# Hybrid attention layer on one core: a weight split, copies, zero fills and the change of branch moved; the last block's exponentials map by map

## The chip, the core and the metric

The kernel runs on one core of a Trainium2 chip. The metric is the device time of one execution in microseconds (us); less is better. The engines are called PE (TensorE), DVE (VectorE), ACT (ScalarE), POOL (GpSimd) and SP (SyncE, which issues most DMAs). Each engine has its own instruction stream, taken in the order written; they meet only at semaphores (`wait_ge`, `then_inc`).

## What is computed

One encoder layer over 1024 tokens of width 1024, in float32. The part that matters here is the input projection and the first of two attention branches (A); the second (B, windowed) follows it at once.

```
h    = layer_norm(x)
proj = h @ w_in                       # qa ka va | qb kb vb | ga gb
# branch A: 8 heads, 2 maps m per head, 8 blocks of 128 queries, chunk-causal
s[m] = q[m] @ k[m]^T * scale + bias ;  s = where(mask, s, -1e30)
p[m] = exp(s[m] - max s[m]) / sum     # one row max and one row sum per map
attn = p[0] - lam * p[1]
o    = attn @ v                       # then a norm per head
# branch B: 16 query heads, 2 kv heads, window of 2 chunks, with sinks
merged = sigmoid(ga)*(ya @ w_branch_a) + sigmoid(gb)*(yb @ w_branch_b)
h = layer_norm(alpha*h + merged @ w_out)
h = layer_norm(alpha*h + relu(h @ w_ff1)**2 @ w_ff2)
```

## The kernel before

Every float32 operand of a matrix product is kept as a high part (rounded copy, made by ACT) and a low part (value minus high part, made by DVE or POOL), and a product is three matmuls: high·high, low·high, high·low (`three`, L588 to L590). The order of each engine's instructions is written out by hand.

**Projection.** `w_in` is taken in tiles of 128 columns (`TILES`: qa, ka, va of head 0, of head 1, ...). A tile needs a split: SP loads `w_raw`, ACT makes the high part (`split_weights` in the scalar block, L892), POOL the low part in four pieces (L1239). A tile has two halves of 512 tokens; each is a `group` of 24 matmuls on PE, which can be issued in two pieces of 12 (`HALVES` says how many pieces lie in a block). ACT and DVE empty the group's PSUM bank (`group_hi`: L910 for q, L914 for k, L921 for v; `qk_lo`, L1409).

**Start.** Tokens are normalised, transposed on PE (`turn_tokens(n)`, L642, n = 0 to 15, two banks), scaled by DVE into `h_full` (`tokens_full`, L1435), and split by ACT (`tokens_hi`, L947) and POOL (L1262, semaphore `h_lo`). PE's first groups wait for `h_lo` piece by piece.

**Branch A.** For head h and block i (step = 8h + i), PE issues: `block_a(0)`, the scores against keys 0 to 511, two maps (L694); one piece of a group of the next head's projection; from i = 4 on `block_a(1)`, the scores against the other keys; the transposes of the probabilities of the step before (`transposes`, L614); the product with v of the step before that (`attend_a`, L677, L678); then perhaps a second piece. One unit of scores is one map and one range of keys; three PSUM banks (`SC`) take the units in turn.

DVE adds the bias and takes the row maxima (L1551, one for each unit), joins the two maxima of a map and negates them (L1561, L1562, semaphore `max_ready`), makes the low part of transposed probabilities (`batch_lo`, L1387), combines the two maps (`combine`, L1525, L1526, L1529, semaphore `probs_ready`, for which PE's transposes wait) and sums the halves of the output (`sum_halves`, L1516). For i > 4 `combine` of the step before stands between the maxima of the first and the second range of keys; the one of i = 7 stands in the next head's block 0, behind its maxima:

```python
                        if c == 0 and i > 4:
                            combine(step - 1)
```

ACT does, in step i, `exp_a(h, i)` (two exponentials with row sums, L1015, semaphore `exp_done`), `group_hi` of the group that ended, `batch_hi` (high part of the transposed probabilities of the step before, L898, semaphore `tr_hi`), and `out_rows` (L1004, L1007). For i < 4 the exponentials come first, for i >= 4 after `batch_hi`:

```python
                    if i < 4:
                        exp_a(h, i)
```

Before the first scores of a head the high part of its queries is copied to the other 64 rows (`double_queries`, L930, semaphore `q_doubled`).

**From A to B.** In the first steps of B the last blocks of A are finished between B's steps. B's values `v_main` and `v_side` need zeros in places, which POOL writes (L1283 and L1299, semaphore `v_zero`), and ACT copies the transposed values (`batch_hi(("vb", 0, b))`).

Of the kernel before, what the change touches and what calls it, by code (L numbers as in the profile page):

```python
# [12 lines left out]
P = 128  # L13
# [115 lines left out]
def program(nc, x, ln_in_g, ln_in_b, rel_bias, w_in, lambda_q1, lambda_k1, lambda_q2, lambda_k2, subln_g, sinks,  # L129
# [6 lines left out]
    with ExitStack() as ctx:  # L136
# [92 lines left out]
        GEMM, SC, TR, PV = banks[0:2], banks[2:5], banks[5:7], banks[7]  # L229
        RING = [banks[2], banks[3], banks[4], banks[7]]  # L230
# [59 lines left out]
        v_zero = sem("v_zero")  # L290
        sink_set = sem("sink_set")
# [293 lines left out]
        def _(pe):  # L585
# [48 lines left out]
            def turn_tokens(n):  # L634

                half, kt = n // KT, n % KT
                if n >= 2:
                    pe.wait_ge(h_full_done, n - 1)
                for t in range(4):
                    if kt == 0:  # L640
                        pe.wait_ge(ln_done, 4 * half + t + 1)
                    mm = pe.transpose(TR[n % 2][:, t * P:(t + 1) * P], res[:, 4 * half + t, kt * P:(kt + 1) * P], ident[:, :])  # L642
                mm.then_inc(h_turned, 1)
# [5 lines left out]
            for n in range(KT):  # L649
                pe.wait_ge(h_lo, n + 1)  # L650
                group(0, 0, [n])
                if n < 4:
                    turn_tokens(n + 4)
            group(1, 0)
            for n in (KT, KT + 1):
                turn_tokens(n)
            for kt in range(0, KT, 2):
                group(2, 0, range(kt, kt + 2))
                turn_tokens(KT + 2 + kt // 2)
            for kt in range(KT):  # L660
                pe.wait_ge(h_lo, KT + kt + 1)
                group(0, 1, [kt])
                if kt < 2:
                    turn_tokens(KT + 6 + kt)
# [16 lines left out]
            for h in range(A_HEADS):  # L681
                at = 0
                for i in range(NT):
# [3 lines left out]
                    def block_a(c):  # L687
                        keys = slice(c * HALF, min((c + 1) * HALF, (i + 1) * P))
                        for m in range(2):
# [43 lines left out]
            def attend_b(s):  # L733
                i = s % NT
                pe.wait_ge(tr_lo, BATCH[("pb", s, 1 if i else 0)] + 1)
                if s == 0:
                    pe.wait_ge(v_zero, 4)
# [144 lines left out]
        def _(act):  # L882
# [98 lines left out]
            for n in range(KT, 2 * KT):  # L981
                tokens_hi(n)
                if n in (KT + 1, KT + 6):
                    group_hi(1 + (n - KT) // 6, 0)
# [34 lines left out]
            double_queries(0)  # L1019
            act.wait_ge(spilled, 16 * NT)  # L1020
            for h in range(A_HEADS):
                at = 0
                for i in range(NT):
                    step = h * NT + i
                    if i < 4:
                        exp_a(h, i)
                    for piece in range(HALVES[i]):
# [4 lines left out]
                        if piece == 0:  # L1032
# [3 lines left out]
                            if i >= 4:  # L1036
# [9 lines left out]
                    splits_at = (1, 4, 5) if h == A_HEADS - 1 else (1, 4, 6)  # L1046
# [22 lines left out]
            for s in range(B_STEPS):  # L1069
                slot, first = s % 2, 0 if s % NT else CHUNK  # L1070
                act.wait_ge(max_ready, A_HEADS * NT + s + 1)
# [159 lines left out]
        def _(pool):  # L1231
# [36 lines left out]
            for n in range(FIRST, TILE[("qb", 1)] + 1):  # L1268
                split_weights(n)
# [105 lines left out]
        def _(dve):  # L1375
# [53 lines left out]
            def tokens_full(n):  # L1429
# [5 lines left out]
                dve.tensor_scalar(h_full[:, n % 4, :], TR[n % 2][:, :], gb_cols[:, kt:kt + 1], gb_cols[:, KT + kt:KT + kt + 1],  # L1435
# [97 lines left out]
            for h in range(A_HEADS):  # L1533
# [4 lines left out]
                for i in range(NT):  # L1538
# [6 lines left out]
                    for c in range(chunks):  # L1545
                        for m in range(2):
# [6 lines left out]
                                                     op0=ALU.add, op1=ALU.max, accum_out=mx[:, slot, m, c:c + 1]).then_inc(scores_read, 1)  # L1553
                        if c == 0 and i > 4:
# [4 lines left out]
                    dve.wait_ge(scores_read, SCORE[("a", h, i, 1, chunks - 1)] + 1)  # L1559
                    if chunks == 2:  # L1560
                        link(dve.tensor_tensor(mx[:, slot, :, 0], mx[:, slot, :, 0], mx[:, slot, :, 1], ALU.max))  # L1561
                    dve.tensor_scalar(neg_max[:, slot, :], mx[:, slot, :, 0], -1.0, None, ALU.mult).then_inc(max_ready, 1)  # L1562
# [31 lines left out]
            for s in range(B_STEPS):  # L1594
# [20 lines left out]
                if s == 0:  # L1615
                    combine(A_HEADS * NT - 1)
# [251 lines left out]
```

## Time and profile before

| | |
|---|---|
| median of 3 runs | 1809.54 us (1808.69 to 1810.73) |
| time of the profiled execution | 1807.46 us |
| its span, first to last instruction | 1805.7 us |
| busy: PE, DVE, ACT, POOL | 1766.9, 1085.4, 743.5, 661.9 us |
| mean granted TensorE clock | 0.997 |
| branch A with the next projections | about 66 to 517 us, 56 us for a head |
| branch B | about 517 to 700 us |

Times inside the execution are microseconds from the start of the span. Busy shares are averages over stages with different limits, so the argument is made from waits and from the order of instructions at one place. A matmul's end is modelled: consecutive matmuls of 512 columns start 0.23 us apart though each is recorded as 0.39 us.

### The profile page before, as it was taken

Reading aid. Unit: us, or ns where it says so; the run is one execution under the profiler, and the core shown is the slowest. Engines: PE = TensorE matmul, PEld = TensorE weight load, DVE = VectorE, ACT = ScalarE, POOL = GpSimd, SP = SyncE. Lnnn points to the kernel's source line nnn. Section 1 sums busy time; section 2 is a strip of 40 time slices with the busy share of each in tenths; the row PEclk is TensorE's granted clock in tenths of the full one; section 3 lists DMA queues with packets and bytes.
Section 4 is the critical chain, followed back from the end, with each engine's and each line's share of the span. In section 5 each row is a group of like instructions: output and inputs, shape, how many; then the busy total and the mean of one; then the engine's idle time right before and its main releaser. Section 6 shows DMA issues by size and latency. Waiting matters only on the chain.

```text
span 1805.7 us, 25434 instructions
## 1 busy us (share of the span) xinstructions
PE 1766.9 (98%) x8815; PEld 1476.3 (82%) x8815; DVE 1085.4 (60%) x2356; ACT 743.5 (41%) x1592; POOL 661.9 (37%) x662
## 2 busy tenths in 40 slices
PE   6999999999999999999999999999999999999998
PEld 4788888888878888888888888788888888888886
DVE  6477777777665553102423574777666667777667
ACT  5466666666556665210221132322233333222232
POOL 4311111121134443222222240555556656555570
PEclk9999999999999999999999999999999999999999
DMA  7311111111121101134232430211211111211212
GB/s 256 127 36 38 44 37 48 37 46 36 34 52 35 33 24 36 47 94 148 97 105 93 152 117 1 82 47 48 68 46 46 46 46 46 69 47 46 65 39 94
DMA packets 143399, 117.91 MB, mean 65 GB/s; under 512 B 23556, under 2 KB 130252, under 8 KB 143308
## 3 DMA queue, kind: packets, MB, share of 16 engines
q1 hardware_dynamic: 134092, 112.52, 20.3%
q10 hardware_dynamic: 9216, 4.20, 0.8%
q8 instruction: 54, 0.88, 0.2%
q14 instruction: 37, 0.30, 0.1%
HBM read 99.88 MB, written 21.53 MB: 67 GB/s over the span
## 4 chain that ended last, share of the span: by engine, by line
PE 88%; DVE 4%; ACT 3%; POOL 2%; issue 2%; DMA 0%; DVEq 0%; ACTq 0%; POOLq 0%
PE bank L588 26%; PE bank L590 26%; PE bank L589 26%; PE bank L614 4%; PE bank L694 3%; PE bank L677 2%; POOL w_lo L1239 1%; PE bank L625 1%; DVE mix L1551 1%; ACT mix L1015 1%; PE bank L678 1%; POOL hT_lo L1262 1%; ACT w_hi L892 1%; DVE mix L1529 0%; DVE small L1416 0%
## 5 line engine op out<-in xcount | busy, mean ns | idle before, releaser
L588 PE MATMUL bank<-hT_hi,w_hi 128*128 128x512 f32 x1296 | 515.1, 397 | 9.5 <-POOL w_lo L1239 4.9
L590 PE MATMUL bank<-hT_hi,w_lo 128*128 128x512 f32 x1296 | 506.8, 391 | 0.0
L589 PE MATMUL bank<-hT_lo,w_hi 128*128 128x512 f32 x1296 | 505.9, 390 | 0.0
L1239 POOL TENSOR_TENSOR w_lo<-w_raw,w_hi 128x256 fp32r<-128x256 f32 x260 | 185.5, 745 | 611.7 <-ACT w_hi L892 611.6
L588 PEld LDWEIGHTS bank<-hT_hi,w_hi 128*128 128x128 f32 x1296 | 244.1, 188 | 64.7 <-POOL hT_lo L1262 7.9
L590 PEld LDWEIGHTS bank<-hT_hi,w_lo 128*128 128x128 f32 x1296 | 243.9, 188 | 52.4
L589 PEld LDWEIGHTS bank<-hT_lo,w_hi 128*128 128x128 f32 x1296 | 244.3, 189 | 47.5
L588 PE MATMUL bank<-y_hi 128*128 128x512 f32 (+1 forms) x548 | 205.9, 376 | 0.8 <-issue 0.8
L589 PE MATMUL bank<-y_lo,y_hi 128*128 128x512 f32 (+1 forms) x548 | 203.2, 371 | 0.0
L590 PE MATMUL bank<-y_hi,y_lo 128*128 128x512 f32 (+1 forms) x548 | 203.2, 371 | 0.0
L1329 POOL TENSOR_TENSOR y_lo<-y_full,y_hi 128x512 fp32r<-128x512 f32 x98 | 131.8, 1373 | 165.9 <-ACT y_hi L1174 165.9
L1737 DVE SCALAR_TENSOR_TENSOR y_full<-bank,y_full 128x512 f32<-128x512 f32 x64 | 44.3, 692 | 187.0 <-ACT y_full L1171 187.0
L1772 DVE TENSOR_TENSOR res<-res,bank 128x512 f32<-128x512 f32 x208 | 132.5, 677 | 0.0
L1333 POOL TENSOR_TENSOR y_lo<-y_full,y_hi 128x512 fp32r<-128x512 f32 x98 | 125.5, 1306 | 16.7 <-DVE y_full L1740 16.7
L1551 DVE CUSTOM_DVE_ANT_0 mix<-bank,aux 128x512 f32<-128x512 f32 (+2 forms) x192 | 99.1, 552 | 48.6 <-PE bank L694 48.1
L1325 POOL TENSOR_TENSOR w_lo<-w_raw,w_hi 128x1024 fp32r<-128x1024 f32 x31 | 79.8, 2575 | 122.1 <-ACT w_hi L1166 122.1
L588 PEld LDWEIGHTS bank<-y_hi 128*128 128x128 f32 x548 | 103.0, 188 | 18.9 <-issue 1.2
L589 PEld LDWEIGHTS bank<-y_lo,y_hi 128*128 128x128 f32 x548 | 103.1, 188 | 17.8
L590 PEld LDWEIGHTS bank<-y_hi,y_lo 128*128 128x128 f32 x548 | 103.0, 188 | 17.8
L1174 ACT ACTIVATE y_hi<-y_full 128x512 fp32r<-128x512 f32 x98 | 54.2, 620 | 147.4 <-DVE y_full L1740 147.4
L1015 ACT ACTIVATE mix<-mix,small 128x256 f32<-128x256 f32 (+7 forms) x128 | 98.2, 769 | 37.7 <-DVE small L1562 36.9
L1740 DVE TENSOR_TENSOR y_full<-y_full 128x512 f32<-128x512 f32 x112 | 111.2, 1013 | 2.1
(202 smaller groups left out, 2992.3 us busy)
## 6 DMA issues: line engine op xcount, KB each, us to landing
w_raw<-in_w_in_dram SPq DMA_DIRECT2D x100, 256.0 KB, 3.3
w_raw<-in_w_ff_dram SPq DMA_DIRECT2D x64, 256.0 KB, 4.1
y_full<-in_w_ff_dram SPq DMA_DIRECT2D x32, 512.0 KB, 3.8
bias_rows<-bias_line SPq DMA_DIRECT2D x3, 1536.0 KB
res<-in_x_dram SPq DMA_DIRECT2D x8, 512.0 KB, 6.5
x_spill<-res SPq DMA_DIRECT2D x8, 512.0 KB, 6.0
o_spill<-o_buf ACTq DMA_DIRECT2D x64, 64.0 KB, 1.6
w_raw<-in_w_branch_b_dram SPq DMA_DIRECT2D x16, 256.0 KB, 3.9
```

Of the source, the lines that this page charges most:

```text
L588: pe.matmul(bank, lhs[0], rhs[0], start=start, stop=False)
L589: pe.matmul(bank, lhs[0], rhs[1], start=False, stop=False)
L590: return pe.matmul(bank, lhs[1], rhs[0], start=False, stop=stop)
L614: mm = pe.transpose(TR[n % 2][:, at * P:(at + 1) * P], src, ident[:, :])
L1015: e = act.activation(s_a[:, i % 2, m, 0:(i + 1) * P], s_a[:, i % 2, m, 0:(i + 1) * P], ACT.Exp, bias=neg_max[:, i % 2, m:m + 1], accum_out ...
L1239: ins = pool.tensor_tensor(w_tile(n, 1)[:, at:at + 2], w_raw[:, at:at + 2, :], w_tile(n, 0)[:, at:at + 2].bitcast(F32), ALU.subtract)
L1325: pool.tensor_tensor(w[1][:, n % 2], w_raw[:, :, :], w[0][:, n % 2].bitcast(F32), ALU.subtract).then_inc(w_lo_done, 1)
L1329: pool.tensor_tensor(w2[1][:, slot, :], w2_full[:, slot, :], w2[0][:, slot, :].bitcast(F32), ALU.subtract).then_inc(w2_lo, 1)
L1333: pool.tensor_tensor(u[1][:, slot, :], u_full[:, slot, :], u[0][:, slot, :].bitcast(F32), ALU.subtract).then_inc(u_lo, 1)
L1551: dve.tensor_tensor_reduce(out=s_a[:, slot, m, lo:hi], in0=SC[n % 3][:, 0:hi - lo], in1=bias_a[:, h % 2, off + lo:off + hi], scale=1.0, sc ...
L1740: dve.tensor_tensor(blocks[:, dst, :], blocks[:, a, :], blocks[:, b, :], op).then_inc(signal, 1)
L1772: ins = dve.tensor_tensor(total, total, bank, ALU.add)
```

## The change

1. **Start.** `turn_tokens` takes four PSUM banks in turn (`TURN = TR + SC[1:3]`) instead of two; in the first group's loop it stands ahead of the wait for `h_lo`, and four turns instead of two stand ahead of group 2. ACT empties group (2, 0) one token tile earlier.
2. **Copies.** `double_queries(0)` moves from behind `group_hi(2, 1)` to behind `group_hi(0, 1)`.
3. **Weight split.** Of the three splits in a head, ACT does the second at the end of block 3 instead of block 4.
4. **Last block of a head (i = 7).** PE issues the first map's second range of scores ahead of the group piece; DVE joins and negates the maxima of each map by itself; ACT's exponentials come at the head of the step, each waiting for its own map.
5. **Zeros.** `v_side[0]` is zeroed by POOL ahead of the split of tile vb, `v_side[1]` by DVE in step 0 of B (semaphore `side_zero`); the two POOL fills between A and B go.
6. **Branch change.** In B's step 1 ACT copies the transposed vb ahead of A's last `out_rows`.

```diff
+        TURN = TR + SC[1:3]
...
-                if n >= 2:
-                    pe.wait_ge(h_full_done, n - 1)
+                if n >= 4:
+                    pe.wait_ge(h_full_done, n - 3)
...
             for n in range(KT):
+                if n < 4:
+                    turn_tokens(n + 4)
                 pe.wait_ge(h_lo, n + 1)
                 group(0, 0, [n])
-                if n < 4:
-                    turn_tokens(n + 4)
...
                     block_a(0)
+                    if i == NT - 1:
+                        block_a(1, [0])
...
                             if i >= 4:
-                                block_a(1)
+                                block_a(1, range(i == NT - 1, 2))
...
             group_hi(0, 1)
+            double_queries(0)
             group_hi(1, 1)
...
             def exp_a(h, i):
-                act.wait_ge(max_ready, h * NT + i + 1)
                 for m in range(2):
+                    act.wait_ge(max_ready, 2 * (h * NT + i) + (m + 1 if i == NT - 1 else 2))
...
-                    if i < 4:
+                    if i < 4 or i == NT - 1:
                         exp_a(h, i)
...
-                            if i >= 4:
+                            if 4 <= i < NT - 1:
                                 exp_a(h, i)
...
-                    splits_at = (1, 4, 5) if h == A_HEADS - 1 else (1, 4, 6)
+                    splits_at = (1, 3, 5) if h == A_HEADS - 1 else (1, 3, 6)
...
                 if s == 1:
+                    act.wait_ge(side_zero, 2)
+                    for b in range(2):
+                        batch_hi(("vb", 0, b))
                     out_rows(A_HEADS * NT - 1, A_HEADS - 1, NT - 1)
                     store_rows(A_HEADS * NT - 1)
-                    act.wait_ge(v_zero, 2)
-                    for b in range(2):
-                        batch_hi(("vb", 0, b))
...
+                if n == TILE[("vb", 0)]:
+                    pool.memset(v_side[0].bitcast(F32), 0.0).then_inc(side_zero, 1)
                 split_weights(n)
...
-            pool.wait_ge(scores_read, SCORE[("b", 0, 0, 0, 0)])
-            for part in range(2):
-                pool.memset(v_side[part].bitcast(F32), 0.0).then_inc(v_zero, 1)
...
+                            if c and i == NT - 1:
+                                dve.wait_ge(scores_read, n + 1)
+                                link(dve.tensor_tensor(mx[:, slot, m, 0:1], mx[:, slot, m, 0:1], mx[:, slot, m, 1:2], ALU.max))
+                                dve.tensor_scalar(neg_max[:, slot, m:m + 1], mx[:, slot, m, 0:1], -1.0, None, ALU.mult).then_inc(max_ready, 1)
...
                 if s == 0:
+                    dve.memset(v_side[1].bitcast(F32), 0.0).then_inc(side_zero, 1)
                     combine(A_HEADS * NT - 1)
```

How the order of instructions moves, at two places. The first is ACT from the last block of head 0 to the first block of head 1 (`w_hi<-w_raw` is a split, `aux_49<-bank` the copy of va's second half, `y_lo<-bank` the two `batch_hi` of block 6, `mix,small<-mix,small` the exponentials, `o_buf` and `unused` `out_rows`). Before:

```order
L892 ACTIVATE w_hi<-w_raw 128x1024 [waits gemm_done,raw_loaded]
L921 ACTIVATE aux_49<-bank 128x512 [waits gemm_done]
L898 ACTIVATE y_lo<-bank 128x512 [waits tr_done]
L898 ACTIVATE y_lo<-bank 128x384 [waits tr_done]
L1015 ACTIVATE mix,small<-mix,small 128x1024 [waits max_ready]
L1015 ACTIVATE mix,small<-mix,small 128x1024
L1004 ACTIVATE o_buf<-o_buf,small 128x128 [waits o_stored1,inv_ready,pv_read]
```

Now:

```order
L894 ACTIVATE w_hi<-w_raw 128x1024 [waits gemm_done,raw_loaded]
L1018 ACTIVATE mix,small<-mix,small 128x1024 [waits max_ready] x2
L923 ACTIVATE aux_49<-bank 128x512 [waits gemm_done]
L900 ACTIVATE y_lo<-bank 128x512 [waits tr_done]
L900 ACTIVATE y_lo<-bank 128x384 [waits tr_done]
L1007 ACTIVATE o_buf<-o_buf,small 128x128 [waits o_stored1,inv_ready,pv_read]
```

The copy of va and both `batch_hi` stand behind the two exponentials, and each exponential has a wait of its own.

The second is DVE at the same place, from the maxima of the second range of keys to the combination of block 7 (`L1551` and `L1552` with `mix,small<-bank` are maxima, `y_lo<-bank,y_lo` the two `batch_lo` of block 6). Before:

```order
L1551 ISA mix,small<-bank,aux_50 128x512 [waits scores_done]
L1551 ISA small 128x1
L1561 TENSOR_TENSOR small<-small 128x2 [waits scores_read]
L1562 TENSOR_SCALAR small<-small 128x2 [waits dve_chain]
L1387 TENSOR_TENSOR y_lo<-bank,y_lo 128x512 [waits tr_hi]
L1387 TENSOR_TENSOR y_lo<-bank,y_lo 128x384 [waits tr_hi]
L1516 TENSOR_REDUCE o_buf<-bank 128x128 [waits sq_done,o_scaled,pv_done]
```

Now:

```order
L1557 TENSOR_TENSOR small<-small 128x1 [waits scores_read]
L1558 TENSOR_SCALAR small<-small 128x1 [waits dve_chain]
L1552 ISA mix,small<-bank,aux_50 128x512 [waits scores_done]
L1552 ISA small 128x1
L1557 TENSOR_TENSOR small<-small 128x1 [waits scores_read]
L1558 TENSOR_SCALAR small<-small 128x1 [waits dve_chain]
L1388 TENSOR_TENSOR y_lo<-bank,y_lo 128x512 [waits tr_hi]
L1388 TENSOR_TENSOR y_lo<-bank,y_lo 128x384 [waits tr_hi]
L1517 TENSOR_REDUCE o_buf<-bank 128x128 [waits sq_done,o_scaled,pv_done]
```

The pair that joins and negates maxima is there twice, one for each map; what follows it (`batch_lo` of block 6, the sum of halves, the next head's first maxima, then `combine` of block 7) keeps its order.

## Rows read from the trace of the kernel before

**Rows 1.** The page: busy time of the engines.
```profile
PE 1766.9 (98%) x8815; PEld 1476.3 (82%) x8815; DVE 1085.4 (60%) x2356; ACT 743.5 (41%) x1592; POOL 661.9 (37%) x662
```
**Rows 2.** PE's waits (line waited at, engine and line that released; total us, times, longest).
```profile
PE bank L588 <- POOL w_lo L1239: 4.9, 8, 0.6
PE bank L588 <- POOL hT_lo L1262: 4.4, 6, 1.4
PE bank L694 <- ACT y_hi L930: 2.9, 1, 2.9
PE bank L614 <- DVE y_lo L1387: 1.4, 2, 1.2
PE bank L614 <- DVE mix L1529: 0.8, 3, 0.3
```
**Rows 3.** PE's timeline, first scores of head 0 (start, length, idle before).
```profile
69.47 0.44 PE L694 MATMUL bank<-y_hi 128*128 128x128 f32 x1 [2.92 <-ACT y_hi L930]
...
74.28 0.28 PE L694 MATMUL bank<-y_hi 128*128 128x256 f32 x1
```
**Rows 4.** One stretch: length, busy (PE, PEld, DVE, ACT, POOL), PEclk, DMA share, GB/s.
```profile
69.40:72.80 3.40, 3.33 (x10) 2.87 (x11) 1.39 (x8) 0.88 (x4) 0.00 (x0) 0.50 0.55 204
```
**Rows 5.** ACT's timeline ahead of the first scores.
```profile
55.70 1.20 ACT L910 ACTIVATE y_hi<-bank 64x512 fp32r<-64x512 f32 x2 [2.37 <-PE bank L590]
61.15 0.59 ACT L914 ACTIVATE y_hi<-bank 64x512 fp32r<-64x512 f32 x1 [4.25 <-PE bank L590]
...
67.21 2.12 ACT L930 ACTIVATE y_hi<-y_hi 64x1024 fp32r<-64x1024 f32 x2
```
**Rows 6.** ACT's timeline, blocks 3 and 4 of head 1.
```profile
153.81 0.60 ACT L898 ACTIVATE p_more<-bank 128x512 fp32r<-128x512 f32 x1 [2.47 <-PE bank L614]
...
156.60 1.05 ACT L892 ACTIVATE w_hi<-w_raw 128x1024 fp32r<-128x1024 f32 x1
```
**Rows 7.** POOL's timeline in the start, second half of the tokens.
```profile
46.23 8.42 POOL L1262 TENSOR_TENSOR hT_lo<-mix,hT_hi 128x256 fp32r<-128x256 f32 x12 [2.04 <-ACT hT_hi L947]
```
**Rows 8.** The timeline, last block of head 1 into head 2.
```profile
177.03 0.68 DVE L1551 CUSTOM_DVE_ANT_0 mix<-bank,aux 128x512 f32<-128x512 f32 x1
177.54 0.98 ACT L898 ACTIVATE y_lo<-bank 128x512 fp32r<-128x512 f32 x2 [0.75 <-PE bank L614]
...
178.25 0.08 DVE L1551 DVE_READ_ACCUMULATOR2_ANT small<- 128x1 f32 x1
...
178.56 0.17 DVE L1562 TENSOR_SCALAR small<-small 128x2 f32<-128x2 f32 x1
178.63 1.15 DVE L1387 TENSOR_TENSOR y_lo<-bank,y_lo 128x512 fp32r<-128x512 f32 x2
...
178.76 1.15 ACT L1015 ACTIVATE mix<-mix,small 128x1024 f32<-128x1024 f32 x1 [0.24 <-DVE small L1562]
...
180.76 0.61 DVE L1562 TENSOR_SCALAR small<-small 128x2 f32<-128x2 f32 x1
...
181.04 0.39 ACT L1004 ACTIVATE o_buf<-o_buf,small 128x128 f32<-128x128 f32 x1
...
181.73 1.42 DVE L1529 SCALAR_TENSOR_TENSOR mix<-mix,small 128x512 f32<-128x512 f32 x2
...
182.53 1.32 PE L614 MATMUL bank<-ident,mix 128*128 128x128 f32 x8
183.22 1.26 ACT L898 ACTIVATE p_more<-bank 128x512 fp32r<-128x512 f32 x2 [0.64 <-PE bank L614]
...
183.86 1.35 DVE L1387 TENSOR_TENSOR p_more<-bank,p_more 128x512 fp32r<-128x512 f32 x2 [0.71 <-ACT p_more L898]
```
**Rows 9.** The timeline, from branch A to branch B.
```profile
514.92 0.95 POOL L1283 MEMSET y_hi<- 128x1024 f32 x1
...
515.04 1.75 DVE L1409 SCALAR_TENSOR_TENSOR y_lo<-bank,y_hi 128x512 fp32r<-128x512 f32 x1
...
516.87 0.33 PE L625 MATMUL bank<-y_hi 64*128 64x128 f32 x2 [0.93 <-DVE y_lo L1409]
```

More of the change, by code:

```diff
@@ L290, in program @@
         v_zero = sem("v_zero")
+        side_zero = sem("side_zero")
         sink_set = sem("sink_set")
@@ L641, in turn_tokens @@
                         pe.wait_ge(ln_done, 4 * half + t + 1)
-                    mm = pe.transpose(TR[n % 2][:, t * P:(t + 1) * P], res[:, 4 * half + t, kt * P:(kt + 1) * P], ident[:, :])
+                    mm = pe.transpose(TURN[n % 4][:, t * P:(t + 1) * P], res[:, 4 * half + t, kt * P:(kt + 1) * P], ident[:, :])
                 mm.then_inc(h_turned, 1)
@@ L649, in _ @@
             for n in range(KT):
+                if n < 4:
+                    turn_tokens(n + 4)
                 pe.wait_ge(h_lo, n + 1)
                 group(0, 0, [n])
-                if n < 4:
-                    turn_tokens(n + 4)
             group(1, 0)
-            for n in (KT, KT + 1):
+            for n in range(KT, KT + 4):
                 turn_tokens(n)
@@ L658, in _ @@
                 group(2, 0, range(kt, kt + 2))
-                turn_tokens(KT + 2 + kt // 2)
+                turn_tokens(KT + 4 + kt // 2)
             for kt in range(KT):
@@ L662, in _ @@
                 group(0, 1, [kt])
-                if kt < 2:
-                    turn_tokens(KT + 6 + kt)
             for n in (1, 2):
@@ L686, in _, with block_a @@
                         pe.wait_ge(q_doubled, h + 1)
-                    def block_a(c):
+                    def block_a(c, maps=range(2)):
                         keys = slice(c * HALF, min((c + 1) * HALF, (i + 1) * P))
-                        for m in range(2):
+                        for m in maps:
                             unit = SCORE[("a", h, i, m, c)]
@@ L736, in attend_b @@
                 if s == 0:
-                    pe.wait_ge(v_zero, 4)
+                    pe.wait_ge(v_zero, 2)
                     pe.wait_ge(pv_read, A_HEADS * NT)
@@ L982, in _ @@
                 tokens_hi(n)
-                if n in (KT + 1, KT + 6):
-                    group_hi(1 + (n - KT) // 6, 0)
+                if n in (KT + 1, KT + 5):
+                    group_hi(1 + (n - KT) // 5, 0)
             act.wait_ge(lam_dve, 1)
@@ L1017, in exp_a @@
                 e.then_inc(exp_done, 1)
-            double_queries(0)
             act.wait_ge(spilled, 16 * NT)
@@ L1070, in _ @@
                 slot, first = s % 2, 0 if s % NT else CHUNK
-                act.wait_ge(max_ready, A_HEADS * NT + s + 1)
+                act.wait_ge(max_ready, 2 * A_HEADS * NT + s + 1)
                 act.wait_ge(sink_set, s + 1)
@@ L1434, in tokens_full @@
                     dve.wait_ge(h_lo, n - 3)
-                dve.tensor_scalar(h_full[:, n % 4, :], TR[n % 2][:, :], gb_cols[:, kt:kt + 1], gb_cols[:, KT + kt:KT + kt + 1],
+                dve.tensor_scalar(h_full[:, n % 4, :], TURN[n % 4][:, :], gb_cols[:, kt:kt + 1], gb_cols[:, KT + kt:KT + kt + 1],
                                   ALU.mult, ALU.add).then_inc(h_full_done, 1)
@@ L1558, in _ @@
                             late = None
[L1559 to L1562, printed above, removed]
+                    if i < NT - 1:
+                        dve.wait_ge(scores_read, SCORE[("a", h, i, 1, chunks - 1)] + 1)
+                        if chunks == 2:
+                            link(dve.tensor_tensor(mx[:, slot, :, 0], mx[:, slot, :, 0], mx[:, slot, :, 1], ALU.max))
+                        dve.tensor_scalar(neg_max[:, slot, :], mx[:, slot, :, 0], -1.0, None, ALU.mult).then_inc(max_ready, 2)
                     if i == 0 and h:
```

## The prediction

> **What bounds the kernel now.** I read the page's busy times first: PE is busy in 1766.9 of 1805.7 us [rows 1], so only about 39 us of idle are there to win, and all the rest can only lose. Then PE's waits [rows 2]: they say which idle belongs to which of the six moves. 4.9 us in 8 waits are for the low part of a weight tile, 2.9 us in one wait for the copied queries, 4.4 us for `h_lo` in the start, 1.4 us for `batch_lo` near the change of branch (and 0.93 us more there [rows 9]), and 0.8 us in all are for `combine` at the ends of heads. Last the timelines at each place, for what stands ahead of and behind the moved instruction. The change aims at every one of these waits; the question is what it puts behind them.
>
> **Copies (part 2).** PE idles 2.92 us until 69.47 for the copies of L930, which ran from 67.21, behind the copy of va [rows 3, 5]. Their input is there after 56.9 us (55.70 + 1.20), and ACT then idles 4.25 us until 61.15 [rows 5]: the 2.12 us fit in whole, and nobody waits behind them. The weights' low part for the next group was ready at about the time PE stopped, so I leave 0.1 us of the wait: -2.8 us. After this gap the granted clock was 0.50 from 69.4 to 72.8 [rows 4], that is 1.2 instead of 2.4 GHz. From 69.47 to the next scores at 74.28 passed 4.81 us [rows 3]; the work between is 4 small and 12 large matmuls, at full clock about 4 x 0.11 + 12 x 0.23 = 3.2 us, so the low clock cost 1.6 us. Without the gap I expect no fall: -1.6. Together **-4.4 us** (bounds -2.8, if the fall comes anyway, and -4.5).
>
> **Weight split (part 3).** The 8 waits of 0.6 us [rows 2] are for a split that ACT begins at 156.60, at the end of block 4 [rows 6]. At the end of block 3 ACT idled 2.47 us until 153.81 [rows 6]; a split takes 1.05 us, so it fits, and POOL's 2.85 us behind it end some 5 us earlier. Its next load on SP's queue also moves earlier. **-4.9 us** (bounds 0, if another wait of PE takes its place, and -4.9).
>
> **Start (part 1).** PE's turns come earlier, but `h_lo` is what PE waits for [rows 2]. POOL makes the second half's low parts without a pause from 46.23 for 8.42 us, 1.4 us for each token tile, after a wait for ACT and not for PE [rows 7]; this run begins behind DVE's low part of group (1, 0), which keeps its place. The first half is held in the same way by DVE's statistics and a weight split. More banks for the turns don't shorten these chains: **0 us** (bounds -1, if DVE gets a turn earlier somewhere, and +1.6, one more fall of the clock, since PE's idle time is then gathered differently).
>
> **Last block (part 4), the term that decides.** The first map's maxima can't start earlier than now: on DVE they stand behind `combine` of block 6, which ends at 177.03 [rows 8], whatever PE does earlier. The pair of small instructions ends 0.40 us after the maxima (178.33 to 178.73) [rows 8]. So map 0 is ready at 177.71 + 0.40 = 178.11 and map 1 at 178.14 + 0.68 + 0.40 = 179.2. The two exponentials take 2.28 us (178.76 to 181.04) [rows 8]; they start at 178.14 and end at 180.42, 0.6 us earlier than now. That is the gain. The price: ACT's copy of va and both `batch_hi` of block 6 now stand behind them, and `batch_hi`, which started at 177.54 [rows 8], starts at 180.42 + 0.5 = 180.9. DVE is in order: its `batch_lo` of block 6, now at 178.63, begins 0.64 us after `batch_hi` (183.22 to 183.86) [rows 8], at 181.55, and the `combine` of block 7 stands behind it. From `batch_lo` to the combining instruction pass 3.10 us now (178.63 to 181.73), of which 0.4 us is one small instruction stretched from 0.17 to 0.61 us while POOL worked [rows 8]; I take 2.7, since POOL's work then lies elsewhere. So combining starts at 184.25 and PE's transposes, 0.80 us behind as now, at 185.05 instead of 182.53: **+2.5 us**. PE has nothing else to do in between: it arrives at these transposes at 182.2 to 182.5 in both programs, and its own stream is in order. The same end of a head comes 7 times: **+17.5 us** (bounds for one: 2.0, if `combine` catches up half a microsecond by not waiting for the exponentials, and 3.0, if the stretched instruction stays).
>
> **The clock behind these stalls.** A gap of 2.92 us was followed by 3.4 us at half clock, costing 1.6 us [rows 3, 4]; each head's end gets one of about 2.8 us. Gaps of up to 1.4 us [rows 2] were mostly not followed by one. I can't tell from one case how many of the seven will be; between none and all I take 3 (they come at changing times, and the one seen was slightly longer): 3 x 1.6 = **+4.8 us** (bounds 0 and 11.2).
>
> **Zeros and branch change (parts 5, 6).** At the end of head 7 DVE's low part of the qb group took 1.75 us beside POOL's zeros of 0.95 us each, and PE waited 0.93 us for it, until 516.87 [rows 9]; the zeros go. But ACT's copy of that same group also stands behind the exponentials now. Map 1 is ready about when L1409 starts now, at 515.04 [rows 9]; the exponentials end 1.2 us behind it (179.2 to 180.42 above), the copy and DVE's low part 1.3 us later (0.6 and 0.7), at 517.5: +0.7. DVE then does the 0.9 us fill of `v_side[1]` (I take POOL's 0.95 us) ahead of `combine` of block 63, for which PE had no wait before: +1.0. Copying vb ahead of `out_rows` saves ACT's 0.8 us of `out_rows` in the longest of the two L1387 waits (1.2 us) [rows 2]: -0.7. Together **+1.0 us** (bounds -1.8, if both old waits go, and +2.5). The fill of `v_side[0]` by POOL lies beside the last head, where DVE has idle time; I take 0 for it. The Trainium skill (SBUF — State Buffer, on the port pair that DVE and GpSimd share) says that the second of two such instructions is blocked for the whole of the first; by it the sum would be up to 0.9 us higher.
>
> **Sum.** -4.4 - 4.9 + 0 + 17.5 + 4.8 + 1.0 = +14.0 us on the profiled execution's 1807.46 us, 1821.5 us. The median of the runs shown is 2.1 us above that execution, so I forecast 1823.6 us.
>
> **Rivals.**
> 1. *Cover: the head ends cost nothing, and the kernel is faster.* Only the gains stay: -4.4 - 4.9, and about -1 at the branch change, 1799 us. For it speaks that exponentials end 0.6 us earlier and that PE's wait there is only 0.8 us in all now [rows 2]. It needs `batch_lo` of block 6 to be no later than about 179 us, that is, `batch_hi` not behind the exponentials. Against it: the listing of ACT's order shows it there, and the same rows show DVE in order. It decides as soon as the added wait of a head's end is under 1.3 us (9.3 / 7). Chance 0.10.
> 2. *Half price.* The wait grows by only 1 to 1.5 us, because DVE's steps between `batch_lo` and `combine` shrink when they no longer wait for anything: 7 x 1.3 = 9, no net change, 1807 to 1815 us. Against it: those steps are mostly work (1.15 us of `batch_lo`, the sum, two maxima, three small ones). Chance 0.10.
> 3. *The clock falls at every head end.* Forecast plus 4 x 1.6 = 1830 us, up to 1834 with 3.0 us a head. For it: the one long gap seen had a fall. Against it: shorter ones mostly had none. Chance 0.18.
> 4. *The split's wait doesn't go* (the raw tile comes too late for block 3): +4.9 on the forecast, 1828 us; the load is issued when POOL ends the split before, some 9 us earlier, and loads take 3.3 us. It lies inside the range; chance 0.05, counted with the forecast.
>
> **How the numbers follow.** The forecast, slower by the head ends, has 0.62; rival 3, 0.18; rival 2, 0.10; rival 1, 0.10. The range from 1813 (head ends at 2.0 us, no fall of the clock, and a little from the branch change) to 1835 (rival 3 with 3.0 us) leaves out rival 1 and most of rival 2. A measurement of this kernel can tell about 0.2%, 3.6 us, from no change. Faster by more: 0.11 (rival 1 and a little of rival 2). Within: 0.06, most of rival 2. Slower by more: 0.83.
>
> **What would show it.** Right: PE's waits list a new large entry, L616 (the transposes) for DVE's L1530, near 18 to 20 us in 7 or 8 waits of 2.5 to 3 us; the entries for POOL's L1239 and ACT's L930 are gone; ACT's `batch_hi` of block 6 starts after the second exponential; the mean clock is a little lower in branch A; head to head takes about 58 us instead of 56. Wrong: head to head takes 55.5 us and L616's wait stays under 1 us, or DVE's `batch_lo` of block 6 starts before 180.5 us on the scale of rows 8.

## The result, and the profile after

The changed kernel took **1820.5 us** (median of 4 runs, 1819.9 to 1824.8) against 1809.8 us for the kernel before on the same chip: ratio 1.0065, 95% interval [1.0047, 1.0082]. The forecast was 1823.6 us, with a range from 1813 to 1835. The profiled execution is the longest of the four: 1824.8 us, with a span of 1823.0 us and a mean granted clock of 0.989, where the others have 0.993 or 0.994. It is +17.3 us on the span of before; the medians differ by +10.7 us. That distance is a finding of its own (below).

The page's busy line, after:

```profile
PE 1775.7 (97%) x8815; PEld 1487.1 (82%) x8815; DVE 1080.4 (59%) x2373; ACT 742.7 (41%) x1592; POOL 660.4 (36%) x661
```

PE has as many matmuls as in [rows 1] and is busy 8.8 us longer. The granted clock, further down, shows where: this execution has 39 us at half clock, the one of before 9 us. PE's waits, after (total us, times, longest):

```profile
PE bank L616 <- DVE mix L1530: 18.6, 7, 2.7
PE bank L644 <- ACT res L944: 7.2, 4, 2.8
...
PE bank L590 <- POOL hT_lo L1264: 3.7, 7, 1.4
PE bank L627 <- DVE y_lo L1410: 1.6, 1, 1.6
```

Against [rows 2]: the 4.9 us for `w_lo` and the 2.9 us for the copies are gone, and 18.6 us for `combine` stand where 0.8 us stood. The timeline at the end of head 1, after (start, length, idle before; the place of [rows 8], where DVE's maxima of the first map began at 177.03):

```profile
174.80 0.68 DVE L1552 CUSTOM_DVE_ANT_0 mix<-bank,aux 128x512 f32<-128x512 f32 x1
...
175.90 1.15 ACT L1018 ACTIVATE mix<-mix,small 128x1024 f32<-128x1024 f32 x1 [5.01 <-DVE small L1558]
...
177.05 1.14 ACT L1018 ACTIVATE mix<-mix,small 128x1024 f32<-128x1024 f32 x1
...
178.18 0.57 ACT L923 ACTIVATE aux<-bank 128x512 f32<-128x512 f32 x1
...
178.66 0.96 ACT L900 ACTIVATE y_lo<-bank 128x512 fp32r<-128x512 f32 x2
...
179.27 1.16 DVE L1388 TENSOR_TENSOR y_lo<-bank,y_lo 128x512 fp32r<-128x512 f32 x2 [2.42 <-ACT y_lo L900]
...
182.03 1.42 DVE L1530 SCALAR_TENSOR_TENSOR mix<-mix,small 128x512 f32<-128x512 f32 x2
...
182.84 1.78 PE L616 MATMUL bank<-ident,mix 128*128 128x128 f32 x8 [2.66 <-DVE mix L1530]
```

Read from the maxima on, since the block as a whole lies at another time: ACT first idles 5.01 us for the first map, then does both exponentials, the copy of va and only then `batch_hi` (L900) (3.86 us behind the maxima; before, 177.54 - 177.03 = 0.51). DVE idles 2.42 us for it, does `batch_lo` (L1388), the sum, the next maxima and `combine` (L1530), and PE's transposes start 8.04 us behind the maxima instead of 5.50: +2.54 us, by the very chain of the prediction. All seven idle times at this place are 2.65 or 2.66 us.

The clock, seven windows of after, one at each head's end (length, busy of PE, PEld, DVE, ACT, POOL, then PEclk):

```profile
121.80:128.60 6.80, 6.19 (x28) 6.10 (x29) 4.33 (x11) 2.31 (x7) 0.00 (x0) 0.50 0.00 0
183.20:186.60 3.40, 3.40 (x18) 3.16 (x17) 2.19 (x6) 1.20 (x2) 0.00 (x0) 0.50 0.02 5
241.90:245.30 3.40, 3.24 (x26) 3.00 (x27) 2.61 (x7) 1.20 (x2) 0.00 (x0) 1.00 0.00 0
299.30:306.10 6.80, 6.28 (x28) 6.18 (x29) 4.33 (x12) 2.22 (x7) 0.00 (x0) 0.50 0.02 5
360.70:364.10 3.40, 3.40 (x18) 3.17 (x16) 2.18 (x6) 1.19 (x2) 0.00 (x0) 0.50 0.00 0
420.00:423.40 3.40, 3.39 (x27) 3.14 (x26) 2.61 (x8) 1.32 (x3) 0.00 (x0) 1.00 0.02 5
476.80:483.60 6.80, 6.30 (x28) 6.21 (x29) 4.33 (x12) 2.19 (x7) 0.00 (x0) 0.50 0.01 4
```

In this execution 5 of the 7 waits have half clock (1.2 GHz) behind them, three of them for 6.8 us. Outside these windows the clock was at half once near 30 us, once at the first scores of B (534.8) and at the very end. What that costs is read from PE's timeline, from the transposes of one head's last block to the next:

```profile
122.41 1.97 PE L616 MATMUL bank<-ident,mix 128*128 128x128 f32 x8 [2.65 <-DVE mix L1530]
...
242.05 1.32 PE L616 MATMUL bank<-ident,mix 128*128 128x128 f32 x8 [2.65 <-DVE mix L1530]
...
360.27 1.78 PE L616 MATMUL bank<-ident,mix 128*128 128x128 f32 x8 [2.66 <-DVE mix L1530]
419.52 1.32 PE L616 MATMUL bank<-ident,mix 128*128 128x128 f32 x8 [2.66 <-DVE mix L1530]
477.30 1.97 PE L616 MATMUL bank<-ident,mix 128*128 128x128 f32 x8 [2.66 <-DVE mix L1530]
```

From 360.27 to 419.52, with 3.4 us of half clock behind the first, pass 59.25 us; from 419.52 to 477.30, with none, 57.78. So a 3.4-us stretch costs 1.5 us. After a 6.8-us stretch (122.41 to the 182.84 above) it is 60.43: 2.7 us. The other heads repeat these three distances within 0.05 us.

### The profile page after: what moved, and what is told of

It is laid out like the page before. It is cut to its first block, busy times and chain, and to the rows that moved or that the text cites. A ratio compares the mean times of both kernels' runs of the same rounds, so it can differ in the third digit from the quotient of the medians.

```text
span 1823.0 us, 25506 instructions
## 1 busy us (share of the span) xinstructions
PE 1775.7 (97%) x8815; PEld 1487.1 (82%) x8815; DVE 1080.4 (59%) x2373; ACT 742.7 (41%) x1592; POOL 660.4 (36%) x661
## 4 chain that ended last, share of the span: by engine, by line
PE 89%; DVE 4%; ACT 3%; issue 2%; POOL 1%; DMA 0%; DVEq 0%; POOLq 0%; ACTq 0%
PE bank L590 26%; PE bank L592 26%; PE bank L591 26%; PE bank L616 4%; PE bank L694 3%; PE bank L677 2%; PE bank L627 1%; ACT mix L1018 1%; PE bank L678 1%; DVE mix L1552 1%; DVE mix L1530 1%; POOL hT_lo L1264 1%; DVE small L1527 0%; DVE y_lo L1388 0%; DVE small L1417 0%
## 5 line engine op out<-in xcount | busy, mean ns | idle before, releaser
L1552 DVE CUSTOM_DVE_ANT_0 mix<-bank,aux 128x512 f32<-128x512 f32 (+2 forms) x192 | 99.6, 552 | 43.8 <-PE bank L694 43.1
L1326 POOL TENSOR_TENSOR w_lo<-w_raw,w_hi 128x1024 fp32r<-128x1024 f32 x31 | 79.8, 2573 | 121.8 <-ACT w_hi L1168 121.8
L591 PEld LDWEIGHTS bank<-y_lo,y_hi 128*128 128x128 f32 x548 | 103.0, 188 | 17.8
L592 PEld LDWEIGHTS bank<-y_hi,y_lo 128*128 128x128 f32 x548 | 102.9, 188 | 17.8
```

The source lines that it names most:

```text
L591: pe.matmul(bank, lhs[0], rhs[1], start=False, stop=False)
L592: return pe.matmul(bank, lhs[1], rhs[0], start=False, stop=stop)
L1326: pool.tensor_tensor(w[1][:, n % 2], w_raw[:, :, :], w[0][:, n % 2].bitcast(F32), ALU.subtract).then_inc(w_lo_done, 1)
L1552: dve.tensor_tensor_reduce(out=s_a[:, slot, m, lo:hi], in0=SC[n % 3][:, 0:hi - lo], in1=bias_a[:, h % 2, off + lo:off + hi], scale=1.0, sc ...
```

## The experiments

Two theories stood against each other. **Theory 1**: the place of the exponentials in ACT's order sends `batch_hi`, then DVE's `batch_lo` and `combine`, then PE back. **Theory 2**: the work map by map does it (DVE's second pair of small instructions, PE's new order). What the other parts are worth was open beside that. Times are medians; ratios are to the kernel before on the same chip, whose median lay between 1809.0 and 1809.7 us.

### Undoing the suspected step, the whole part, and doing the part alone

`exp_behind`, the change with the exponentials of i = 7 behind `batch_hi` again and all else of part 4 kept:

```diff
-                    if i < 4 or i == NT - 1:
+                    if i < 4:
                         exp_a(h, i)
...
-                            if 4 <= i < NT - 1:
+                            if i >= 4:
                                 exp_a(h, i)
```

> The changed kernel with one thing undone: in a head's last block ACT does both exponentials behind the copies of the transposed probabilities again; the maxima are still joined map by map and PE still issues the first map's second scores early. Theory 1 (the price is the place of the copies behind the exponentials on ACT, and DVE's low parts behind them): PE's 7 waits of 2.7 us for the combined probabilities shrink to 0.4 us or less, the clock falls after them go, and the time is 1797 to 1801 us. Theory 2 (the price is DVE's added pair of small instructions, or PE's changed order, which let the maxima end later): the waits stay above 1.5 us and the time stays above 1812 us.

Measured: **1796.7 us**, ratio 0.9934 [0.9917, 0.9950], 24 us faster than the change and a little below the expected 1797. The waits at the heads' ends are 0.43 to 0.74 us, a little more than the 0.4 us expected; the one of 1.1 us in the row below lies at the change of branch, behind DVE's fill. `no_last`, the change without part 4 (those lines, PE's `block_a(1, [0])`, and DVE's pair for each map undone):

> The changed kernel without any of part 4 (last block as before: PE's order, joined maxima and exponentials), parts 1, 2, 3, 5 and 6 kept. Both theories: faster than before by the sum of the other parts. By the prediction's terms -4.4 (copies), -4.9 (split), 0 (start) and about -1.7 (zeros and branch change without the exponentials): 1809.8 - 11 = 1799 us, 1797 to 1802. The difference between this run and the one with the exponentials behind the copies says what joining map by map is worth by itself: theory 1 says under 1 us either way, theory 2 says 10 us or more.

Measured: **1795.9 us**, ratio 0.9925 [0.9909, 0.9942]; a second time, as `no_last_again`, 1794.7 us, 0.9917 [0.9903, 0.9930]. Both lie below the expected 1797 to 1802: the other parts are worth more than was thought. `last_only`, the kernel before with part 4 and nothing else:

> The kernel before with part 4 alone. Theory 1: 7 waits of 2.6 to 2.7 us instead of 0.8 us in all (+17 us), a later first score of branch B (+1 us), and falls of the granted clock at some of the heads' ends (+5 to +11 us): 1833 to 1839 us. If the clock has nothing to do with these waits, 1827 to 1829 us.

Measured: **1839.2 us**, ratio 1.017 [1.0137, 1.0202], at the upper end of what was expected. Part 4 costs 30 us here and 25 us in the change; one difference is the wait for `w_lo`, which grew from the 4.9 us of [rows 2] to 6.5 us. PE's waits of `exp_behind` and of `last_only`, a row of each:

```profile
PE bank L616 <- DVE mix L1530: 4.2, 7, 1.1
```
```profile
PE bank L614 <- DVE mix L1531: 18.6, 7, 2.7
```

So Theory 1 holds: two lines in ACT's order carry 24 of the 25 us, and the same 18.6 us of wait come back in a kernel with nothing but part 4. The timeline of `exp_behind` at the end of head 1 shows what the exponentials' early place had won:

```profile
170.33 0.68 DVE L1552 CUSTOM_DVE_ANT_0 mix<-bank,aux 128x512 f32<-128x512 f32 x1
...
170.85 0.98 ACT L900 ACTIVATE y_lo<-bank 128x512 fp32r<-128x512 f32 x2 [0.29 <-PE bank L616]
...
171.71 1.15 ACT L1018 ACTIVATE mix<-mix,small 128x1024 f32<-128x1024 f32 x1
...
172.84 1.15 ACT L1018 ACTIVATE mix<-mix,small 128x1024 f32<-128x1024 f32 x1
...
176.16 1.32 PE L616 MATMUL bank<-ident,mix 128*128 128x128 f32 x8 [0.43 <-DVE mix L1530]
```

From the maxima to the end of the second exponential pass 172.84 + 1.15 - 170.33 = 3.66 us here and 177.05 + 1.14 - 174.80 = 3.39 us in the change. The early place wins 0.27 us on exponentials that nobody waits for at this point, and makes `batch_hi` 3.34 us later. `batch_hi` itself, ahead of the exponentials, lies almost wholly in the time in which DVE makes the first map's maximum: it holds the first exponential back by those 0.3 us.

### How much wait for how much delay

`one_ahead`, the change with the first map's exponential at the head of step 7 and the second behind `batch_hi`:

```diff
-            def exp_a(h, i):
-                for m in range(2):
+            def exp_a(h, i, maps=range(2)):
+                for m in maps:
...
-                e.then_inc(exp_done, 1)
+                if m:
+                    e.then_inc(exp_done, 1)
...
-                    if i < 4 or i == NT - 1:
+                    if i < 4:
                         exp_a(h, i)
+                    if i == NT - 1:
+                        exp_a(h, i, [0])
...
-                            if 4 <= i < NT - 1:
-                                exp_a(h, i)
+                            if i >= 4:
+                                exp_a(h, i, [1] if i == NT - 1 else range(2))
```

> The changed kernel with the second map's exponential of the last block moved behind the copies of the transposed probabilities, and the first map's left ahead of them: one of two steps of what stood in front. If the added wait is the length of what stands ahead of the copies on ACT (theory 1), one exponential of 1.15 us less in front but the second one then ending later gives 7 waits of 1.2 to 1.6 us instead of 2.7, and with gaps that short the granted clock falls at fewer heads or none: 1804 to 1810 us. If the price comes all at once with any work ahead of the copies, the waits stay near 2.7 us and the time near 1820.

Measured: **1805.5 us**, ratio 0.9982 [0.9972, 0.9991]. The end of head 1, and the window behind it:

```profile
174.01 0.97 ACT L900 ACTIVATE y_lo<-bank 128x512 fp32r<-128x512 f32 x2
...
178.21 1.32 PE L616 MATMUL bank<-ident,mix 128*128 128x128 f32 x8 [1.53 <-DVE mix L1533]
```
```profile
178.20:181.60 3.40, 3.39 (x27) 3.15 (x28) 2.61 (x7) 1.20 (x2) 0.00 (x0) 1.00 0.02 5
```

One exponential (1.15 us) taken from ahead of `batch_hi` shortens PE's wait by 1.13 us (2.66 to 1.53): the chain passes ACT's delay on one for one. None of the seven waits of 1.5 us had half clock behind it in the profiled execution, and in all ten runs the mean clock was 0.997 to 0.999, where the change has 0.989 to 0.994. The kernel gains 15 us on the change, and 7 x 1.13 us is 8. The other 7 fit the stretches at half clock that are gone; the parts were not timed apart.

`pe_order_back`, the change with PE's order of before (both maps' second range behind the group piece):

```diff
-                    if i == NT - 1:
-                        block_a(1, [0])
...
-                                block_a(1, range(i == NT - 1, 2))
+                                block_a(1)
```

> The changed kernel with PE's part of the last block undone: both maps' second scores behind the group piece, as before. My reading of the timeline says that DVE reaches those scores only when it has combined block 6, after PE has made them in either order, so nothing moves: 7 waits of 2.7 us, 1819 to 1825 us like the change. If PE's order is part of the price, 3 us or more faster; if it is what lets the exponentials start, slower.

Measured: **1826.4 us**, ratio 1.0094 [1.0077, 1.0110], above the expected 1819 to 1825. The wait stays:

```profile
PE bank L616 <- DVE mix L1528: 18.6, 7, 2.7
...
PE bank L627 <- DVE y_lo L1408: 2.2, 1, 2.2
```

PE's new order does not cause the wait. The row for the first scores of B is 0.6 us longer than in the change. The medians are 6 us apart, but the clock is too: all four runs here have a mean clock of 0.990 or 0.991, three of the four of the change 0.993 or 0.994. Its one run at 0.989 took 1824.8 us, 1.6 us less than this median. So at a like clock PE's new order seems to be worth 1 to 3 us; one run of the change at that clock is thin evidence. What else the medians show fits the difference in clock.

### The other parts one by one

`copies_only`, the kernel before with part 2:

> The kernel before with part 2 alone (the copy of head 0's queries earlier). If the fall of the clock at 69.4 us came from PE's gap of 2.92 us there: -2.8 (the wait) and -1.6 (the low clock), 1805.4 us. If the clock would fall there anyway: 1807 us.

Measured: **1805.1 us**, ratio 0.9973 [0.9961, 0.9984], so between -2.9 and -7.1 us, and -4.4 us by the medians. The wait at L694 is gone and there is no half clock near 69 us. But that fall did not come every time before either: five traces have this wait of 2.92 us, and two of them (the kernel before and `zeros_only`) have half clock behind it; `split_only`, `start_only` and `last_only` have none. `split_only`, the kernel before with part 3:

> The kernel before with part 3 alone (the second split of a head at the end of block 3). By the prediction's term -4.9 us: the 8 waits of 0.6 us go, 1804.7 us. If the 0.6 us that PE lost in block 5 were what kept it from waiting at the head's end, part comes back there as waits for the combined probabilities: 1806 to 1807 us.

Measured: **1801.8 us**, ratio 0.9967 [0.9955, 0.9978], so -6 us (-4.0 to -8.1). No row for `w_lo` is left among PE's waits. What goes beyond -4.9 does not come from ACT behind the split's old place: the copy there (L898) starts 1.31 us earlier (158.09 instead of 159.40), but the one ahead of it, 153.81 in [rows 6], is already 1.30 us earlier:

```profile
152.51 0.60 ACT L898 ACTIVATE p_more<-bank 128x512 fp32r<-128x512 f32 x1 [1.52 <-PE bank L614]
```

The profiled execution is 7.6 us below the one of before. Of that 4.9 are the wait, 1.1 are waits for `h_lo`, and about 1.5 are the half clock at 69 us, which this trace lacks though its wait of 2.92 us is still there. So the size beyond -4.9 is not shown to belong to the split. `zeros_only`, the kernel before with parts 5 and 6:

> The kernel before with parts 5 and 6 alone (zero fills and the order at the change of branch). Without the exponentials in front the waits of 0.9 and 1.2 us at the change of branch go, DVE's fill of 0.9 us comes in front of the combination of A's last block: -1 to -2 us, 1808 to 1809 us. It is too small to be told from no change by the times; the waits in the profile decide.

Measured: 1808.6 us, ratio 0.9994 [0.9984, 1.0004], no difference that could be told, as expected. Its timeline at the change of branch:

```profile
521.02 0.91 DVE L1616 MEMSET y_lo<- 128x1024 f32 x1 [0.16 <-issue]
522.25 1.42 DVE L1529 SCALAR_TENSOR_TENSOR mix<-mix,small 128x512 f32<-128x512 f32 x2
...
523.72 0.55 PE L615 MATMUL bank<-ident,mix 128*128 128x128 f32 x3 [1.24 <-DVE mix L1529]
```

DVE's fill stands ahead of `combine` of block 63, and PE waits 1.24 us where it had no wait. Against that the 0.93 us of [rows 9] are gone, and the wait for L1387 fell from 1.4 to 0.3 us. The other kernels with parts 5 and 6 agree: the wait behind the fill (1.06 to 1.32 us) is there in all that keep full clock at this place, and absent in the change and in `pe_order_back`, whose clock is at half there. `start_only`, the kernel before with part 1:

> The kernel before with part 1 alone (turns of tokens over four banks, four of them ahead of group 2, group (2, 0) emptied one tile earlier). Theory 1 (the chains of the start are set by POOL's low parts and DVE, not by banks): within 1 us of before, POOL's run of twelve low parts starts within 0.5 us of 46.2. Rival (PE now fills gaps that it waited in): 2 to 4 us faster, PE's wait L588 for hT_lo falls from 4.4 to 2 us or less. Rival (the clock falls once more in the start): 1 to 2 us slower.

Measured: 1806.8 us against 1809.7, ratio 0.9989 [0.9980, 0.9998], 0.4 to 3.6 us faster, more than the 1 us expected. PE's waits give no reason for it:

```profile
PE bank L589 <- POOL w_lo L1238: 5.1, 8, 0.8
PE bank L589 <- POOL hT_lo L1261: 4.8, 8, 1.4
PE bank L693 <- ACT y_hi L929: 2.9, 1, 2.9
```

They are as long as before. POOL's timeline does give one. Its run of twelve low parts was expected within 0.5 us of the 46.23 of [rows 7], and starts 1.4 us earlier:

```profile
44.82 8.37 POOL L1261 TENSOR_TENSOR hT_lo<-mix,hT_hi 128x256 fp32r<-128x256 f32 x12 [2.04 <-ACT hT_hi L946]
```

Among traces with the same length of half clock ahead of it, the run is earlier wherever part 1 is there: with 3.4 us it starts at 46.23 to 47.47 without part 1 and at 45.38 to 46.15 with it; with 6.8 us at 48.59 (`zeros_only`) and at 47.07 (`pe_order_back`).

The clock differs too. In the profiled execution of `start_only` (clock 0.999) it fell nowhere ahead of the last 5 us, though the gap of 2.9 us at L693 is there, behind which [rows 4] shows half clock. Near 32 us all five traces without part 1 have half clock, and three of the eight with it have none. The eleven runs have mean clocks of 0.996 to 0.999 and their times follow: 1805.4 to 1806.8 us in the four runs at 0.998, where the five of the kernel before at 0.998 took 1807.0 to 1810.5. So some 1 to 2 us seem to be there at a like clock too, about what the start's chain gains. Which of the moves inside part 1 shortens it, and whether part 1 also spares the fall near 32 us, stays open.

### A version that beats both

`split5` is `no_last` with the third split at the end of block 5 in every head:

```diff
-                    splits_at = (1, 3, 5) if h == A_HEADS - 1 else (1, 3, 6)
+                    splits_at = (1, 3, 5)
```

> The same kernel as no_last (the change without part 4), beside the next one on the same chip. Near 1796 us.

> The change without part 4, and in every head the third split at the end of block 5 instead of 6 (in the change that is so only in the last head). Theory: POOL's split then no longer runs beside DVE's combine of block 6 and ACT has less work ahead of block 7, so what is left of PE's wait L616 for combine (2.0 us in no_last) shrinks to under 1 us: 1 to 2 us faster than no_last_again. Rival: the raw tile isn't there yet at block 5, or POOL's low part only moves its load to another place: no difference within 0.1%, or an entry for w_lo L1241 of some tenths of a us for each head.

Measured: **1792.1 us**, ratio 0.9900 [0.9885, 0.9915], 2.6 us below the 1794.7 us of `no_last_again` on the same chip (the intervals of the two overlap a little), where 1 to 2 us were expected. PE's waits for `combine`, of `no_last_again` and of `split5`:

```profile
PE bank L616 <- DVE mix L1528: 2.3, 4, 1.2
```
```profile
PE bank L616 <- DVE mix L1528: 1.2, 1, 1.2
```

The small waits of the heads' ends are gone, and the one of 1.2 us that stays is as long as the one `zeros_only` has behind DVE's fill, and lies at the same place; so the row does not fall under the 1 us that was expected. Why the others are gone, the two instructions of `combine` of block 6 in head 1 show, in `no_last` and in `split5`:

```profile
168.90 1.71 DVE L1528 SCALAR_TENSOR_TENSOR mix<-mix,small 128x512 f32<-128x512 f32 x2
```
```profile
167.96 1.28 DVE L1528 SCALAR_TENSOR_TENSOR mix<-mix,small 128x512 f32<-128x512 f32 x2
```

With the third split at block 6, POOL's low parts (166.71 to 169.54) run beside it; with the split at block 5 they are over at 163.19. The small instruction ahead of it goes from 0.81 to 0.22 us. The wait went down by 1.1 us, the spans by 1.3; the rest of the 2.6 us is within the spread of both kernels' runs (2.2 and 2.5 us).

## Why the prediction was right, and where its terms were off

**Last block** (7 x 2.5 = +17.5, the term that decides): the entry is 18.6 us less the 0.8 us of before, +17.8. For head 1 each step was right as well: exponentials first, copy of va, `batch_hi` 3.86 us behind the maxima (predicted 180.9 - 177.03 = 3.87), the transposes +2.54 us. The gain was sized at 0.6 us and is there: from the maxima to the end of the second exponential pass 3.39 us instead of 181.04 - 177.03 = 4.01. Of these 0.62 us the exponentials' place is worth 0.27, by `exp_behind`; the rest comes from doing the maps one by one.

**Clock** (3 x 1.6 = +4.8): this term was too small. Fewer waits were expected to be followed by half clock, and none for longer than 3.4 us. The profiled execution had 5 of 7, three of them with twice the length: 2 x 1.5 + 3 x 2.7 = 11.1 us. Over all runs: the change is 25.2 us slower than `no_last` (1820.5 against 1795.3, the mean of its two medians), of which PE's wait for `combine` is 18.6 - 2.2 = 16.4 us, which leaves about 8.8 us, between the 4.8 of the forecast and the 11.2 of rival 3 (a fall at every head's end), and nearer to the rival. In the profiled execution it is 12.6 us (29.0 us between the spans of the change and of `no_last`, less 16.4), with the fall at the first scores of B. For the time as a whole, 1820.5 is nearer to the forecast than to the rival's 1830.

**Copies** (-4.4): measured -4.4 by the medians. The 2.8 us of the wait are sound. The 1.6 us for the clock are partly luck: the fall is there in 2 of 5 traces with this wait, so the copies can be credited with about 0.6 us of it in the mean (an estimate, 2/5 of 1.5), and the interval (-2.9 to -7.1) holds that sum as well. **Weight split** (-4.9): measured about -6, with -4.9 inside the interval of -4.0 to -8.1. **Start** (0): -0.4 to -3.6 alone. This term was wrong in its reason too: it held that more banks don't shorten POOL's chain, and POOL's second run starts 1.4 us earlier in `start_only` and 0.85 us earlier (45.38) in the change.

**Zeros and branch change** (+1.0): alone between -2.9 and +0.7 us. The +1.0 holds 0.7 us that only the exponentials bring, so the like term is +0.3, inside that interval. In the change the first scores of B had the predicted +0.7 (1.6 us of wait instead of 0.9), and L1388 gained 1.1 us where 0.7 was predicted. The step that did not hold for the change is DVE's fill as a wait of PE: it is there in `zeros_only` (1.24 us), and in the whole change no wait stands at this place. There the clock was at half from 534.8, so that PE, slower with its own work ahead of the transposes, covers the fill.

The fill of `v_side[0]` by POOL was taken at 0, and the trace of the change bears that out. It lies beside `combine` of block 6 in the last head:

```profile
467.62 1.71 DVE L1530 SCALAR_TENSOR_TENSOR mix<-mix,small 128x512 f32<-128x512 f32 x2
468.19 0.96 POOL L1272 MEMSET y_hi<- 128x1024 f32 x1
```

This `combine` takes 1.71 or 1.72 us in the heads before as well, where POOL's low parts overlap it in the same way and no fill follows them; the maxima come at once behind it. By the rule on the port pair (the Trainium skill, SBUF — State Buffer, Who interferes with whom) the fill could have held DVE for up to 0.9 us, but only an instruction of DVE in a 2-port mode: one with two SBUF inputs, as `combine` is, contends with a POOL instruction that reads SBUF and not with one that only writes it. The trace agrees. The two old fills did hold DVE in the trace of before: a small instruction of DVE (L1562), 0.17 us in [rows 8], took 1.82 us beside them:

```profile
514.97 1.82 DVE L1562 TENSOR_SCALAR small<-small 128x2 f32<-128x2 f32 x1
```

The low part behind it (L1409), whose 1.75 us the prediction put down to the fills, ends together with it at 516.79; in `zeros_only` it takes 0.68 us.

**The sum**: parts 1, 2, 3, 5 and 6 together are `no_last`, -13.5 to -15 us on before. The sum has -8.3 for them, or -9.0 without the 0.7 us that the exponentials bring at B's first scores. So they are worth 4.5 to 6 us more than forecast; the split's 1.1, the start's 1 to 3 and the branch change's 1.4 (+0.3 forecast, about -1.1 measured) account for most of it. Part 4 with its clock is 25.2 us, where 23.0 were forecast. The total landed within 3.1 us of the forecast because these errors have opposite signs. The mechanism of the deciding term was right; that the total came so near was in part luck. Rival 1 (cover) and rival 2 (half price) fell: the added wait is 2.5 us at each head's end. Rival 2's size, a wait of 1 to 1.5 us more at each head, is what `one_ahead` has.

## What to carry to other kernels

An instruction moved to the head of a step on an engine that works in order delays whatever stood there. Before such a move, ask of both: who waits for it, and how long does it wait for its own input? Here ACT's exponentials and `batch_hi` become ready within a microsecond of each other: PE's transposes for `batch_hi` end about 0.3 us before the first exponential starts. Whichever is written first goes first, and only `batch_hi` led the chain to PE. With the exponentials first it stood 3.3 us later. A stall can cost more than its own length: in the change five of seven stalls of 2.66 us had half clock behind them, which cost another 1.5 or 2.7 us each. So when several parts are measured as one change, time each alone: five of these six were worth -14 us together, and one edit of two lines hid that.

## What was not expected of the hardware

After the seven waits of 2.66 us the clock was at half five times in the change, and five times of seven in `pe_order_back` and, at other heads, in `last_only`; after seven waits of 1.53 us (`one_ahead`), never. But length alone does not set it: the wait of 2.92 us at the first scores of head 0 had half clock behind it in two traces of five. And at the first scores of B the clock fell behind a wait of 1.59 us, at 534.8, with matmuls of only 64 rows and 128 columns next to it; in `last_only` and `pe_order_back` it did the same, behind 1.59 and 2.23 us.

In all thirteen traces the stretches at half clock were 3.4 or 6.8 us, nothing between, but for the last one, which the end of the execution cuts short. In the change the three long ones began 0.5 to 0.6 us ahead of PE's first instruction after the wait (121.8 for 122.41, 299.3 for 299.82, 476.8 for 477.30); the two short ones began 0.4 us behind it (183.2 for 182.84, 360.7 for 360.27). The other two traces agree on the long ones (0.5 to 0.7 us ahead of PE); their short ones began 0.3 to 1.7 us behind. The same stall thus costs 0, 1.5 or 2.7 us more. The Trainium skill (TensorE: Matmul & The Clock Gate, Part 1) says that the chip watches PE's activity at a beat of its own, which doesn't start anew with the kernel; the change agrees, with one stall and three outcomes in one execution. That the moment of the stall decides which outcome comes was not tested by a run.

So the mean clock has to be read with every time. `last_only` took 1834.6 us at 0.994 and 1846.9 us at 0.986, with the same instructions: about 1.5 us for each thousandth, the rounding of the printed clock. And one profiled execution is no measure of the median: 4.3 us above it for the change, 2.3 us below it for the kernel before.
